# Inverse roots of q and k per tile, and other slots for layer norm, state-space steps and silu, in a one-core hybrid decoder block in float32

## The reference, cut to what matters

```
h = rms_norm(x);  ca, cg, q, k, v, iq, ik, iw, z, xbc, dt = split(h @ w_in)
u = silu(layer_norm(causal_dwconv31(ca * sigmoid(cg))))        # 512 channels
q, k = rms_norm over each head's 64 columns (8 heads)
att = softmax over the 128 best keys of each query, chosen by an indexer; @ v
xbc = silu(causal_dwconv4(xbc));  y = chunked state-space scan(xbc, dt) + skip
y = rms_norm(y * silu(z))
x = x + concat(u, att, y) @ w_out
x = x + (silu(fg) * fa) @ w_down,   fa, fg = split(causal_dwconv3(rms_norm(x) @ w_up))
```

## Time and profile before

| | |
|---|---|
| median of three executions | 790.46 us |
| the profiled execution | 790.41 us |
| its span, first to last instruction | 788.7 us |
| PE busy | 738.3 us (94%) |
| PE weight load busy | 588.2 us (75%) |
| DVE busy | 478.9 us (61%) |
| ACT busy | 338.8 us (43%) |
| POOL busy | 91.7 us (12%) |
| mean granted TensorE clock | 0.969 |
| chain that ended last | PE 72%, DVE 10%, issue 8%, ACT 4%, POOL 4% |

### The profile page before, as it was taken

How to read it: one execution, slowest core, us unless ns; L and a number is a source line. 1 busy time by engine, 2 the same in 40 slices (tenths; PEclk the granted TensorE clock), 3 DMA queues, 4 the chain that set the end, 5 groups by cost and what they waited for, 6 DMA issues and landing times.

```text
span 788.7 us, 9486 instructions
## 1 busy us (share of the span) xinstructions
PE 738.3 (94%) x3442; PEld 588.2 (75%) x3446; DVE 478.9 (61%) x725; ACT 338.8 (43%) x508; POOL 91.7 (12%) x75
## 2 busy tenths in 40 slices
PE   3999978599989989799997999999999999999998
PEld 2766757477766778587875888888888888888886
DVE  5246797996799866666655565655656656222222
ACT  6244637187855576263334334344343443211110
POOL 2000364753100001303010000000000000000000
PEclk9999998799999999999996999999999999999999
DMA  8431132222211141102231133233332332333202
GB/s 260 151 139 55 54 106 54 54 62 91 63 53 54 55 160 54 53 16 92 81 108 53 54 106 84 78 105 106 106 96 74 96 106 106 107 106 107 82 26 106
DMA packets 78047, 69.46 MB, mean 88 GB/s; under 512 B 5815, under 2 KB 64535, under 8 KB 78015
## 3 DMA queue, kind: packets, MB, share of 16 engines
q1 hardware_dynamic: 77871, 68.51, 28.2%
q10 hardware_dynamic: 144, 0.52, 0.2%
HBM read 66.91 MB, written 2.12 MB: 88 GB/s over the span
## 4 chain that ended last, share of the span: by engine, by line
PE 72%; DVE 10%; issue 8%; ACT 4%; POOL 4%; DMA 1%; SPq 0%; DVEq 0%; POOLq 0%; ACTq 0%
PE bank L1454 62%; PE bank L1460 3%; POOL stats L730 3%; DVE u_acc L569 2%; PE bank L1474 2%; DVE w_lo L579 1%; DMA x_in<-in_x 1%; PE bank L1649 1%; PE bank L1625 1%; PE bank L1592 1%; DVE xbcT L1261 1%; DVE q_tok L1224 1%; POOL u_acc L751 1%; DVE k_tok L1224 1%; DVE h_lo L1090 1%
## 5 line engine op out<-in xcount | busy, mean ns | idle before, releaser
L1454 PE MATMUL bank<-h_hi,w_hi 128*128 128x512 f32 x480 | 191.3, 398 | 1.8 <-DVE h_lo L1090 1.8
L1454 PE MATMUL bank<-h_lo,w_hi 128*128 128x512 f32 x480 | 188.0, 392 | 0.0
L1454 PE MATMUL bank<-h_hi,w_lo 128*128 128x512 f32 x480 | 188.0, 392 | 0.0
L579 DVE TENSOR_TENSOR w_lo<-w_raw,w_hi 128x2048 fp32r<-128x2048 f32 x34 | 78.6, 2312 | 80.7 <-ACT w_hi L820 80.7
L1454 PEld LDWEIGHTS bank<-h_hi,w_hi 128*128 128x128 f32 x480 | 90.7, 189 | 28.4 <-issue 9.9
L1454 PEld LDWEIGHTS bank<-h_hi,w_lo 128*128 128x128 f32 x480 | 90.7, 189 | 19.6
L1454 PEld LDWEIGHTS bank<-h_lo,w_hi 128*128 128x128 f32 x480 | 90.9, 189 | 18.1
L1415 DVE SCALAR_TENSOR_TENSOR f<-bank,prm,f 128x511 f32<-128x511 f32 x88 | 65.8, 748 | 58.3 <-ACT f L1059 52.0
L820 ACT ACTIVATE w_hi<-w_raw 128x2048 fp32r<-128x2048 f32 x34 | 64.9, 1910 | 78.3 <-PE bank L1454 78.0
L1059 ACT ACTIVATE f<-bank,prm 128x512 f32<-128x512 f32 x44 | 33.8, 769 | 102.4 <-PE bank L1454 102.4
L1454 PE MATMUL bank<-w_hi,g_hi 128*128 128x512 f32 x176 | 68.5, 389 | 0.0
(11 more groups left out here) (231 smaller groups left out, 1049.8 us busy)
## 6 DMA issues: line engine op xcount, KB each, us to landing
w_raw<-in_w_up SPq DMA_DIRECT2D x44, 512.0 KB, 4.7
w_raw<-in_w_in SPq DMA_DIRECT2D x34, 512.0 KB, 4.6
w_raw<-in_w_down SPq DMA_DIRECT2D x22, 512.0 KB, 4.0
w_raw<-in_w_out SPq DMA_DIRECT2D x12, 512.0 KB, 4.3
x_in<-in_x SPq DMA_DIRECT2D x4, 512.0 KB, 6.8
trev<-distance_table SPq DMA_DIRECT2D x1, 2048.0 KB, 8.0
x<-in_x SPq DMA_DIRECT2D x4, 512.0 KB, 6.8
out_x<-y_out SPq DMA_DIRECT2D x8, 256.0 KB, 2.0
```

Source lines behind the costliest of these rows:

```text
L579: eng.tensor_tensor(wlo[:, slot, cols], wraw[:, slot, cols], whi[:, slot, cols].bitcast(F32), ALU.subtract).then_inc(ready, 1)
L1454: ins = pe.matmul(o, a, b, start=first and i == 0 and q == 0, stop=last and i == n - 1 and q == 2)
```

## The change

The scaling of the sums, the root and the multiplication of q and k become one step per tile of 128 tokens: `qkms` moves to the fill of slots 17 to 20 (q) and 25 to 28 (k), `qkn` to the front of slots 19 to 22 and 27 to 30. The arithmetic is the same; POOL raises 8 columns to the power -0.5 eight times instead of 32 columns twice. Convolution tiles 1, 2 and 3 end in slots 50, 63 and 65. `ln` moves to slots 66, 66, 67, 67, `lnT` to 70, 70, 71, 71, the four state-space chunks start two slots later, `silux` and `cs` move from slot 62 to 64, `xt` from 63 to 65, `siluz` from 68 to 70.

```diff
-DW_SLOTS = [(15, 44), (14, 52), (42, 66), (46, 69)]
-LN_SLOT = 69
-SSD_SLOTS = (66, 70, 74, 78)
+DW_SLOTS = [(15, 44), (14, 50), (42, 63), (46, 65)]
+LN_SLOTS = (66, 66, 67, 67)
+LNT_SLOTS = (70, 70, 71, 71)
+SSD_SLOTS = (68, 72, 76, 80)
...
         for t in range(NT):
             put(n + 1 + t, ("qkev", what, t))
-        fill[n + 4].append(("qkms", what))
-        front[n + 7].append(("qkn", what))
+            fill[n + 1 + t].append(("qkms", what, t))
+            front[n + 3 + t].append(("qkn", what, t))
...
-    d2 = LN_SLOT
     for t in range(NT):
-        put(d2 + 1 + t // 2, ("ln", t))
-        front[d2 + 2 + t // 2].append(("lnn", t))
+        put(LN_SLOTS[t], ("ln", t))
+        front[LN_SLOTS[t] + 1].append(("lnn", t))
     for j in range(4):
-        put(d2 + 4 + j // 2, ("lnT", j))
+        put(LNT_SLOTS[j], ("lnT", j))
...
-    s0 = at[("z", 0)] + 2
+    s0 = at[("z", 0)] + 4
     put(s0, ("silux",), ("cs",))
...
-    put(at[("z", 1)] + 4, ("siluz",))
+    put(at[("z", 1)] + 6, ("siluz",))
...
                 elif k == "qkms":                                   # POOL
-                    which = "qk".index(s[1])
-                    pool.wait_ge(qkms_ready, which + 1)
-                    inverse_root(rqk[:, 32 * which:32 * which + 32],
-                                 ssqk[:, 32 * which:32 * which + 32], rqk_ready)
+                    i = NT * "qk".index(s[1]) + s[2]
+                    pool.wait_ge(qkms_ready, i + 1)
+                    inverse_root(rqk[:, NH * i:NH * i + NH], ssqk[:, NH * i:NH * i + NH], rqk_ready)
...
                 elif k == "qkms":                                   # DVE
-                    dve.wait_ge(sq_used, NT * (w + 1))
+                    dve.wait_ge(sq_used, i + 1)
-                    c = ssqk[:, 32 * w:32 * w + 32]
+                    c = ssqk[:, NH * i:NH * i + NH]
                     dve.tensor_scalar(c, c, a, b, ALU.mult, ALU.add).then_inc(qkms_ready, 1)
                 elif k == "qkn":
-                    dve.wait_ge(rqk_ready, w + 1)
-                    for t in range(NT):
-                        v3 = tok[:, t, :].rearrange("p (h c) -> p h c", h=NH)
...
+                    dve.wait_ge(rqk_ready, i + 1)
+                    v3 = tok[:, t, :].rearrange("p (h c) -> p h c", h=NH)
+                    dve.tensor_tensor(v3, v3, rqk[:, NH * i:NH * i + NH].unsqueeze(2)
+                                      .to_broadcast([P, NH, HD]), ALU.mult).then_inc(qkn_ready, 1)
```

More of the change, by code:

```diff
@@ L1209, in _ @@
                 elif k == "qkms":
-                    w = "qk".index(s[1])
-                    dve.wait_ge(sq_used, NT * (w + 1))
+                    i = NT * "qk".index(s[1]) + s[2]
+                    dve.wait_ge(sq_used, i + 1)
                     a, b = (1.0, HD * EPS) if s[1] == "q" else (1.0 / HD, EPS)
-                    c = ssqk[:, 32 * w:32 * w + 32]
+                    c = ssqk[:, NH * i:NH * i + NH]
                     dve.tensor_scalar(c, c, a, b, ALU.mult, ALU.add).then_inc(qkms_ready, 1)
                 elif k == "qkn":
-                    w = "qk".index(s[1])
-                    tok = q_tok if s[1] == "q" else k_tok
-                    dve.wait_ge(rqk_ready, w + 1)
-                    for t in range(NT):
-                        v3 = tok[:, t, :].rearrange("p (h c) -> p h c", h=NH)
-                        c = 32 * w + NH * t
-                        dve.tensor_tensor(v3, v3, rqk[:, c:c + NH].unsqueeze(2)
-                                          .to_broadcast([P, NH, HD]), ALU.mult).then_inc(qkn_ready, 1)
+                    _, what, t = s
+                    i = NT * "qk".index(what) + t
+                    tok = q_tok if what == "q" else k_tok
+                    dve.wait_ge(rqk_ready, i + 1)
+                    v3 = tok[:, t, :].rearrange("p (h c) -> p h c", h=NH)
+                    dve.tensor_tensor(v3, v3, rqk[:, NH * i:NH * i + NH].unsqueeze(2)
+                                      .to_broadcast([P, NH, HD]), ALU.mult).then_inc(qkn_ready, 1)
                 elif k == "logit":
```

## The result

The changed kernel takes 778.18 us (median of four executions, 775.79 to 778.26); the kernel before, beside it on the same chip, 789.62 (788.63 to 791.02). The ratio is 0.9847, 95% interval 0.982 to 0.9873: 1.5% faster, well clear of 1, and the median is the predicted time to 0.1 us.

The account below looks back on a forecast made before the run. PE was held mainly by DVE: scaling q and k (stops of 7.8 and 8.3 us, then half clock), layer norm, and pace from 203 to 245 us. -8.5 + 2.7 + 0.5 - 7.0 = -12.3 against 790.41: 778.1 us, range 772 to 785.

Parts of the forecast that it names:

- Part 1: Scaling q and k tile by tile ends the long waits before their transposes: -8.5 us, ends -3 and -13.
- 2.3 us more: Behind k's transposes: PE also saves 2.3 us of transposes and matmuls that ran at half clock after the old stop.
- 3.2 us for half clock behind the two new stops: Slots 24 and 32: PE loses 1.6 us behind each new stop of about 3 us, +3.2 us in all.
- Part 2: Earlier convolution taps load DVE, without slack up to slot 53, by four taps of 0.70 us: +2.7 us, ends 0 and +5.6.
- Part 3: Silux two slots later: probT's 2.1 us wait goes, waits for xt (0.7) and xs (2.2) come: +0.5 us, -1.5 to +2.5.
- Part 4: Layer norm earlier, state space later: both 2.7 us waits and 1.6 us behind them go, -7.0 us; other end -2.
- A: POOL and ACT's loop: roots beside lo last 4.1 us, not 2.1; q and k bring only -3.5; 783.1 us; chance 0.20.
- D: Roots shut DVE out: eight waits up to 2.1 us, q and k bring nothing or +4; 786.6 to 790.6; chance 0.04.
- B: DVE bounds up to slot 63: earlier taps cost 5.6 us, layer norm and state space bring only 4; 784.0; chance 0.10.
- C: Root paid by instruction, not column: 7.4 us for 8 columns in q and k; slower, 811.6 us; chance 0.05.
- E: New stops before slots 24 and 32 vanish, so scaling q and k brings -13; 773.6 us; chance 0.12.
- F: PE is so full that all gain is given back in the dense stretch; 790 us; chance 0.02.

Follow-up runs that it names:

- Taps only: Kernel before with only the changed kernel's earlier convolution tap slots (DW_SLOTS); 791.68 us, ratio 1.0031.
- changed again: The changed kernel measured once more without any edit, on another chip; 777.38 us, ratio 0.9851 to the kernel before.
- Silux only: Kernel before with only silux, cs and xt two slots later; 788.27 us, ratio 1.001.
- q and k only: Kernel before with only the roots and multiplications of q and k per tile, all slots as before; 781.26 us, ratio 0.9907.
- slots only: Kernel before with only the moved slots (taps, layer norm, state space, silux, cs, xt, siluz), roots as before; 783.78 us, ratio 0.9933.
- three variants: Changed kernel with dwp a slot later (0.9822); with tile 1's taps over slots 20 to 50 (0.9897); with search, silux and tile 1 moved, dwp not (0.9794).
- The four small moves of slots together: Changed kernel with dwp a slot later, silux and cs in slot 63, tile 1's taps over slots 20 to 58, block 1's search over 9 to 17; 768.55 us, 0.9754.
- the run with the search early: Changed kernel with block 1's search over slots 9 to 17 instead of 9 to 36; 774.67 us, ratio 0.9821.
- dwp a slot later: Changed kernel with ACT's products for the taps of tile 0 spread over slots 15 to 44, not 14 to 43; 774.26 us, ratio 0.9822.

## Why the prediction was right

**Part 1, -8.5 forecast, -7.1 to -7.8 measured.** The mechanism held step by step: root of 8 columns 2.1 us, stops before slots 24 and 32 of 2.47 and 2.16 us (2.9 and 3.1 forecast), q's transposes at 116.7 (117.0), k's at 145.6 (145.9); as the start was 1.3 us early, both ran about a microsecond behind the plan. What failed is the step that PE keeps what it has gained at k's transposes and 2.3 us more. The prediction followed DVE up to the fourth multiplication and stopped there; it saw DVE without slack from 203 to 245 us only. Logit 0, 15.5 us of DVE work from that multiplication on, took 3.2 us back, and half clock behind it 1.6 in one of two profiles. The sum came out near by luck: the forecast had added 3.2 us for half clock behind the two new stops, on top of k's start, where it came once and not twice (slot 24 in one profile, slot 32 in the other) and within the time up to k's transposes. Less the early start these come 8.4 us sooner (9.4 forecast), about 2 us of slow matmuls go (2.3), and in place of the 3.2 of half clock stand the 3.2 of logit 0.

**Part 2, +2.7 forecast.** Taps only: +2.4 by the ratio, +1.9 in the rest, of which 2.0 by slot 53. Size and place are right, and DVE's added work there, 1.75 us, is the cause given. The sign named for it, waits for `probT` up by 2 to 3 us, came in the first profile of the changed kernel (+2.3 between 203 and 256 us) but not in changed again or taps only (+0.8): there half clock behind the longer wait made up the time.

**Part 3, +0.5 forecast.** Silux only: within the noise, -1.1 in the rest of its trace. This is mostly half clock that has nothing to do with silux: the sixteen transposes of slot 63 happened to take 3.45 us at half clock in the profile of the kernel before, and 2.06 in q and k only, where silux stays in its place too. From slot 62 to 66 silux only takes 17.9 us, q and k only and taps only 17.2, so that +0.7 is nearer for the move itself. The exchange of one wait for the other came as worked out, 2.44 us at the fourth transpose where 2.2 was said; the wait of 0.7 at `xt` did not come. Both figures lie in the ends of -1.5 and +2.5.

**Part 4, -7.0 forecast.** From slot 66 to the feed-forward part -8.6 us in the first profile, -7.0 in changed again and in slots only (115.1 and 115.2 against 122.1). The difference between them is again one slot at half clock, slot 66 behind the stop for `xs_tok`. Here is the chain over slots 66 and 67 in the changed kernel:

```profile
296.11 2.78 PE bank L1452 x12
298.89 0.88 PE bank L1458 x8
299.76 2.74 PE bank L1452 x12
302.50 0.87 PE bank L1458 x8
...
306.11 0.23 PE bank L1668
```

The eight transposes of `ln` follow the matmuls without a gap, and `csr` finds its bank; before, it stood 2.7 us and the slot behind took 4.34.

**The rivals.** A asked for roots of 4.1 us: the longest in the changed kernel is 2.68. Its mechanism, POOL's part of the loop held up by DVE's `w_lo`, did come, at the tap beside the root (4.36 us). In three variants it came at a root too (4.22 and 4.68 us), once in each and not two or three times; so its price per root was about right, and it was closer than the changed kernel alone shows. D expected `w_lo` and multiplications to wait for roots; in the changed kernel none did. But the prediction went too far when it took one `w_lo` at its usual length inside a root as a sign that the two do not contend: in those three variants `w_lo` kept its 2.3 us and the root paid. And the Trainium skill (SBUF — State Buffer, Who interferes with whom) says in so many words only of VectorE's two-port modes that the later one is blocked for the whole instruction; of two SBUF inputs it says that they contend. B is refuted by taps only. C fell with the first root. E said that the new stops vanish; they did not. F is refuted by the result; but that DVE gives back in a dense stretch what PE gains is what the second score shows, in an earlier stretch than those I had looked at.

The 0.1 us between forecast and median is partly luck: part 1 was some 1 us too good, part 2 about 0.5 too bad, the feed-forward part brought 0.6 that no part has, and single slots at half clock and the start vary by more.

## What to carry to other kernels

After a long stop is taken away, follow each engine that took part in it beyond the point where the gain is booked, up to the next place where PE needs its result: here 15.5 us of gapless DVE work from the last multiplication on took 3 of 9 us back. Count the work between the last event for which that engine waits anyway and the result that is needed; what lies before that event is free for that result, what lies behind it is not, so that fewer taps in all, but one more in that piece, made the wait 0.6 us longer. Before two edits in one stretch are said to need or to replace each other, take the slots at half clock out of both: here the gains then about added up. The four small moves of slots together gave 1% more, the best single one half of that.

## What was not expected of the hardware

**Half clock after the same stop, or not.** Two executions of the same code: in the first, slot 36 behind the wait for logit 0 is at half clock for most of it (the row of 4.54 us above, granted clock 0.68 over its first 3 us) and slot 32 is not (3.03 us from first to last matmul, granted clock 1). In changed again it is the other way round, by the chain of this run:

```profile
161.70 2.95 PE bank L1452 x12
```

That is slot 36, behind a stop of 2.93 us; slot 32, behind one of 2.15 us, took 4.61 there (granted clock 0.63). So 1.6 us behind a stop of 2 to 3 us is a price that is sometimes paid; several such stops make a scatter of a few us between executions.

**POOL gives way to DVE at one time and not at another.** The same kind of tap took 4.36 us beside a multiplication and `w_lo` that kept their times, and in the run with the search early 1.48 us, while the multiplication beside it took 1.56 instead of 0.69:

```profile
140.86 1.48 POOL L750 TENSOR_TENSOR u_acc<-xskip,u_acc 128x499 f32<-128x499 f32 x1
```

Roots do the same. The two roots shown with dwp a slot later have the multiplication 0.16 us ahead of them and `w_lo` 0.43 us behind their start, in both runs to 0.01 us, and one takes 2.02 us, the other 4.22. So which of the two pays, and 2 to 3 us of the path with it, is not read off the order of starts. What decides it was not tried by itself and stays open.
